# Starting places of TensorE's rounded moving operands: bytes 48, 40, 16 and 48 of a 64-byte line in place of 32

## The reference

```python
x = x + 0.5 * swiglu(rms_norm(x, g), w_gu, w_down)       # four times, 1024 -> 2 x 2816 -> 1024
x = x + even_mixer(rms_norm(x, g), ...)                  # h @ w_in, attention, a gated recurrence, @ w_out
x = x + odd_mixer(rms_norm(x, g), ...)                   # h @ w_in, sparse attention, @ w_out
x = x + sigmoid(rms_norm(x, g) @ gate) * (p @ w_in)      # twice
p = rms_norm(x, g) @ w_in                                # 1024 -> 11520, then convolutions, scans, a recurrence
x = x + m @ w_out
x = x + square(relu(rms_norm(x, g) @ w1)) @ w2           # 1024 -> 4096 -> 1024
```

## Time and profile before

| | |
|---|---|
| median of 3 runs | 1747.99 us |
| the runs | 1743.96, 1749.81, 1747.99 us |
| span of the profiled execution | 1751.1 us |
| TensorE busy | 1694.5 us, 97% of the span |
| weight loads busy | 1574.0 us, 90% |
| VectorE, ScalarE busy | 1290.8 us (74%), 995.2 us (57%) |
| mean granted TensorE clock | 0.982 of full speed |
| transfers | 278 MB, 159 GB/s |

### The profile page before, as it was taken

How to read it: one execution, slowest core, us unless ns; L and a number is a source line. 1 busy time by engine, 2 the same in 40 slices (tenths; PEclk the granted TensorE clock), 3 DMA queues, 4 the chain that set the end, 5 groups by cost and what they waited for, 6 DMA issues and landing times.

```text
span 1751.1 us, 37772 instructions
## 1 busy us (share of the span) xinstructions
PE 1694.5 (97%) x14502; PEld 1574.0 (90%) x14502; DVE 1290.8 (74%) x2137; ACT 995.2 (57%) x1562; POOL 3.0 (0%) x9
## 2 busy tenths in 40 slices
PE   7999999999999999999999999989999999899998
PEld 6999899889999989999988999989999998798887
DVE  6777867658777887777767777877788774567776
ACT  5544655445444664445555554668877875444444
POOL 0000000000000000000000000000000000000000
PEclk9999989899999999999999999999999999999999
DMA  6555533115555445554425655545555550055554
GB/s 230 191 188 183 165 133 109 62 31 181 192 191 188 162 166 192 180 191 157 145 82 173 192 188 188 169 157 184 178 183 191 175 163 4 23 174 179 186 187 144
DMA packets 75864, 278.24 MB, mean 159 GB/s; under 512 B 8432, under 2 KB 8688, under 8 KB 75248
## 3 DMA queue, kind: packets, MB, share of 16 engines
q1 hardware_dynamic: 75168, 273.58, 47.9%
q0 software_dynamic: 592, 3.15, 0.5%
HBM read 274.59 MB, written 2.10 MB: 158 GB/s over the span
## 4 chain that ended last, share of the span: by engine, by line
PE 83%; DVE 8%; ACT 6%; issue 2%; DMA 0%; DVEq 0%; SPq 0%; ACTq 0%
PE ps L475 82%; DVE w_lo L464 2%; ACT w_hi L456 2%; PE ps L2471 1%; DVE rstd L607 1%; DVE x L943 1%; DVE h L568 1%; DVE arena L911 0%; DVE arena L915 0%; ACT L2796 0%; ACT L2780 0%; DMA x<-x_t 0%; DVE arena L656 0%; DVE a_lo L931 0%; ACT arena L2133 0%
## 5 line engine op out<-in xcount | busy, mean ns | idle before, releaser
L475 PE MATMUL ps<-h,w_hi 128*128 128x256 f32 (+1 forms) x3380 | 732.4, 307 | 0.0
L464 DVE TENSOR_TENSOR w_lo<-raw,w_hi 128x1024 fp32r<-128x1024 f32 x514 | 621.4, 1215 | 86.6 <-ACT w_hi L456 67.5
L456 ACT ACTIVATE w_hi<-raw 128x1024 fp32r<-128x1024 f32 x514 | 538.6, 1050 | 223.2 <-PE ps L475 205.6
L475 PE MATMUL ps<-h,w_lo 128*128 128x256 f32 x2026 | 583.9, 289 | 22.9 <-DVE w_lo L464 15.6
L475 PEld LDWEIGHTS ps<-h,w_hi 128*128 128x128 f32 x3380 | 554.4, 193 | 26.4
L475 PEld LDWEIGHTS ps<-h,w_lo 128*128 128x128 f32 x2026 | 390.5, 193 | 30.1 <-DVE w_lo L464 14.5
L475 PE MATMUL ps<-h_of_feed_forward,w_hi 128*128 128x512 f32 (+1 forms) x1088 | 351.5, 374 | 0.0
L475 PE MATMUL ps<-h_of_feed_forward,w_lo 128*128 128x256 f32 x1000 | 278.8, 281 | 0.8 <-issue 0.6
L896 ACT ACTIVATE arena<-ps 128x256 f32<-128x256 f32 x208 | 79.1, 382 | 267.7 <-PE ps L475 267.7
L475 PEld LDWEIGHTS ps<-h_of_feed_forward,w_hi 128*128 128x128 f32 x1088 | 198.3, 188 | 36.3
L475 PE MATMUL ps<-a_hi,w_lo 128*128 128x256 f32 x776 | 218.3, 281 | 4.2 <-DVE a_lo L931 4.2
(11 more groups left out here) (354 smaller groups left out, 1447.9 us busy)
## 6 DMA issues: line engine op xcount, KB each, us to landing
raw<-weights SPq DMA_DIRECT2D x514, 512.0 KB, 3.4
con<-shape_constants SPq DMA_DIRECT2D x1, 1618.0 KB, 10.5
x<-x_t SPq DMA_DIRECT2D x1, 1024.0 KB, 5.0
stored<-x POOLq DMA_DIRECT2D x1, 1024.0 KB, 4.8
x<-stored POOLq DMA_DIRECT2D x1, 1024.0 KB, 7.9
out_t<-arena SPq DMA_DIRECT2D x4, 256.0 KB, 2.1
arena<-p_t POOLq DMA_DIRECT2D x2, 256.0 KB, 4.1
arena<-final_gain POOLq DMA_DIRECT2D x1, 512.0 KB, 4.6
```

The lines of the kernel that those rows point to most:

```text
L456: A.activation(w_hi[:, u % RING, 0:n], raw[:, u % RING, 0:n], ACT.Copy).then_inc(s_hi, 1)
L464: V.tensor_tensor(w_lo[:, u % RING, 0:n], raw[:, u % RING, 0:n], f(w_hi[:, u % RING, 0:n]), SUB)\
L475: return TE.matmul(o, lhsT, rhs, start=start, stop=stop, skip_group_check=True)
```

## The change

Four operands are moved by some bytes; no instruction is added, removed or reordered.

- `h` becomes a flat tensor with 8 floats more, and the view that is used starts at its fifth float: 48 in place of 32. The room behind it shrinks from 88 floats to 80, so that `raw`, `w_hi` and `w_lo` stay where they were.
- `a_hi` and `a_lo` become flat tensors with 8 floats more, each used from its fifth float; `in_front_of_a` goes. `a_hi` starts at 16 and `a_lo` at 48 in place of 32.
- All that stands behind them (parameters, constants, `rstd`, `arena`) moves on by 32 bytes, so `arena` and the constants start at 0 in place of 32.
- `h_two`: the lower part of `arena` gives up 8 floats, which takes back those 32 bytes, and the view starts at the third float: 40 in place of 32.

```diff
-        h = sbr("h", [P, KT, 2, T])
+        h = sbr("h", [P, KT * 2 * T + 8])[:, 4:4 + KT * 2 * T].rearrange("p (k a t) -> p k a t", k=KT, a=2)
         h_hi, h_lo = h[:, :, 0, :], h[:, :, 1, :]
-        sb("behind_h", [P, 88])
+        sb("behind_h", [P, 80])
         raw = sb("raw", [P, RING, UNIT])
         w_hi, w_lo = sbr("w_hi", [P, RING, UNIT]), sbr("w_lo", [P, RING, UNIT])
-        sb("in_front_of_a", [P, 8])
-        a_hi, a_lo = sbr("a_hi", [P, 3, T]), sbr("a_lo", [P, 3, T])
+        a_hi, a_lo = (sbr(name, [P, 3 * T + 8])[:, 4:4 + 3 * T].rearrange("p (b t) -> p b t", b=3) for name in ("a_hi", "a_lo"))
...
-        with nc.sbuf_tensor("lower_arena", [P, 8192], f32), \
-                nc.sbuf_tensor("h_of_feed_forward", [P, KT, 2, T], mybir.dt.float32r) as h_two:
+        with nc.sbuf_tensor("lower_arena", [P, 8184], f32), \
+                nc.sbuf_tensor("h_of_feed_forward", [P, KT * 2 * T + 8], mybir.dt.float32r) as h_moved:
             pass
+        h_two = h_moved[:, 2:2 + KT * 2 * T].rearrange("p (k a t) -> p k a t", k=KT, a=2)
```

## The result

The changed kernel takes 1761.02 us in the median of four runs (1760.18 to 1763.95); the kernel before, on the same chip, 1746.10 (1743.96 to 1749.81). The ratio is 1.0085, 95% interval 1.0068 to 1.0102: 14.9 us slower. The forecast was 1739.8 us with a range up to 1756; it fell on the wrong side, outside the range.

What follows compares the result with a forecast made beforehand. TensorE, busy 97% of the span, was taken as the bound. Savings of 4.9 us (`h`), 2.4 (second `h`) and 1.9 (`a`), together 9.1, passed on at nine tenths as 8.2, gave 1739.8 us from 1747.99; range 1726 to 1756 us.

Steps and rivals of the forecast that it cites:

- 11406 portions: Moving reads on `h`, second `h` and `a`, counted per 256 columns; one nanosecond each is 11.4 us, or 0.65%.
- the excess: TensorE's 9 to 12 ns per 256 columns beyond the 106.7 ns for columns, laid to TensorE's own reads.
- DVE's cast: Cast into `a_hi`, 294 ns; losing its faster way would cost 15.7 us of DVE; taken as 0.
- the nine tenths assumed: Share of TensorE's 9.1 us gain reaching the end, 8.2 us, because TensorE waits for split units or activations.
- between -2.0 and +2.0 ns: Bounds on the change in cost per 256 columns moved from `h`, second `h` or `a`, sign open.
- I take -0.8 ns: Chosen saving per 256 columns for moving reads of `h`, second `h` and `a`, together 9.1 us.
- Later in the line is cheaper: Moving operands starting later in a 64-byte line cost less; applied strictly, it gave 5.5 us in all.
- The third case: Moving reads: half a line is the best place, so the change loses time, 1756 to 1760 us; chance 0.21.
- an extra 16-byte piece: Second `h` at 40 touches 65 pieces per tile in place of 64, 1.8 ns a read, 3.8 us.
- The place doesn't matter: Rival: moving operands' start bytes leave matmul cost unchanged, so time is 1748 us; chance 0.32.
- The floor of 108.8 ns: Spacing of one-column matmuls with full stationary slices; threes can fall at most 9 ns of 118.
- the even hump: Moving-read cost highest at byte 0, falling evenly towards 32 from both sides, 1.6 ns for the whole way.

## Why the prediction was wrong

**What held.** That TensorE's spacing is what the change moves, that 11406 portions make one nanosecond 11.4 us, that the other engines don't set the excess, and that the moved scratch, DVE's cast (294 ns, 120 times, before and after the earlier trace rows) and the waits cost nothing in the change. That much of a change in spacing reaches the end: the sums of spacing were 17.1 us for the change, 12.5 for everything at 0 and -8.7 for `h` at 192 (`h` -10.6 and +4.2, `a` -2.1, weights -0.3), the times 14.9, 10.8 and -8.0. That is 0.86 to 0.92, near the nine tenths assumed; but over all eight kernels that ran repeatedly the share goes from 0.55 (the change with its second `h` put back, 4.5 of 8.2 us) to 1.0 (only the second `h`). The assumed cause, waits, isn't the whole of it. In the run with 0.55 the granted clock was 0.9869 on the mean against 0.9846 for the kernel before, which is worth 4.0 us; with these the 4.5 are 8.5. Why the clock differs is not shown. With `h` at 192 both were at work: TensorE stood idle for 60.0 us in place of 56.6, and the clock (0.9870) gave 4.3 us back. That the size per portion lay between -2.0 and +2.0 ns held for `h` (+1.2 and +1.1) and `a` (+0.8), not for the second `h`: a pair with 8.7 ns more is 2.9 per portion.

**The step that failed** is the reading of the earlier trace rows as "a start at byte 0 against a start at byte 32", and with it the sign in "I take -0.8 ns" (measured per portion: 0.8 to 2.9 ns more). In those rows weights move and an activation is stationary. The text named this as another difference and used the rows all the same. By the runs, what counts is not the start over 64 bytes but where the moving operand lies relative to the stationary one, over a multiple of 256 bytes, and the pattern in which the stream starts. Measured so, the change put `h` from 160 to 176 behind the weights, second `h` from 160 to 168, `a_hi` from 32 to 16 and `a_lo` from 32 to 48. "Later in the line is cheaper" had no footing: over 256 bytes the pairs on `h` or second `h` read 347.3 ns at 32, 349.2 at 64, 354.5 at 104, 351.0 at 128, 346.9 at 160, 355.8 at 168, 350.0 at 176, 353.2 at 192 and 347.8 or 353.4 at 224. Where several runs share a distance other than 224, they agree to within 1.1 ns. No interpolation between two points of that row is worth anything; 8 bytes made 8.7 ns.

**The rivals.** The third case had the sign and nearly the time (1756 to 1760 us for 1761.0), by a mechanism that fell: it gave `h` and `a` 6.7 us, and they took 9.0; it gave second `h` 1.2, or 5.0 with an extra 16-byte piece, and it took 8.3; for everything at 0 it gave 24 us for 10.8 measured. That its time was nearly right is luck. "The place doesn't matter" is wrong, but its remark stands that two stretches of `linear` at one place differ by 1.6 ns, which fits patterns: in the kernel before, threes on `h` run from 349 to 362 ns. The floor of 108.8 ns from matmuls of one column isn't far: the best threes, 340.0 ns, are 113.3 a matmul.

**The range** ended at 1756 us, at half of the way back to 0 by the even hump. With no row at any of the new places, the bound per portion had to come from the whole spread of spacing in the trace, and in the third case the second `h` was charged with the least per portion because it moved least, which nothing in the trace supported.

**What stays open.** Why a distance of 256 bytes closes the cycle, what in a pattern stalls the stream, and what chooses between patterns besides the places in the stream ahead. Since a pattern can be worth 5.6 ns a pair (at 224), part of a difference between two distances can be a pattern too. The place of `a` was never timed alone at the change's own addresses; its 1.9 us rests on the spacing.

## What to carry to other kernels

When two operands of one instruction are read at the same time, state a placement by their distance, not by the address of one, and before comparing two streams in a trace, check that the same operand moves in both. A spacing that depends on the layout is to be measured at each candidate over the whole period; it doesn't interpolate, and padding in front of one tensor shifts all behind it. Where the operands of the stream ahead lie counts as well, and even one layout can give two spacings, so look at the spread of turns, not only at their mean.

## What the runs showed of the hardware

- With 4-byte rounded operands at a granted clock of 1.00, matmuls of 256 columns that each load a 128 x 128 slice are 113.3 to 120.2 ns apart (mean threes of 340.0 to 360.7), pairs of 256 and 512 columns 347 to 356 ns, by layout alone.
- The spacing follows the distance from the stationary to the moving operand; the same distance with both moved gave 350.4 and 350.7 ns, a distance changed by moving the weights 350.4 for 351.0 ns. It repeats after 256 bytes (353.2 and 353.2 ns; 347.2 and 347.1), not after 64 or 128.
- At one distance a stream can run in two repeating patterns, 340 and about 353 ns a three, or 347 and 353 a pair, and keeps the one it has started in. Which one depends in part on the operands of the stream ahead: pairs on an unmoved `h` took 347.9 or 353.5 ns by the place of `a`, threes on an unmoved `a` 350.4 or 353.3 ns by the place of the second `h`.
